# Expert feed-forward on one core: the gate times its sigmoid in one ScalarE function instead of a ScalarE sigmoid and a VectorE product

## What is computed

```
gu = xe @ w_gate_up[e] + b_gate_up[e]
gate, up = jnp.split(gu, 2, axis=-1)
gate = jnp.minimum(gate, SWIGLU_LIMIT)            # 7.0
up = jnp.clip(up, -SWIGLU_LIMIT, SWIGLU_LIMIT)
act = gate * jax.nn.sigmoid(SWIGLU_ALPHA * gate) * (up + 1)   # alpha = 1.702
y = act @ w_down[e] + b_down[e]
```

## Time and profile before

| | |
|---|---|
| time, median of 3 runs | 2448.58 us (2444.11 to 2453.59) |
| profiled execution, own time | 2447.04 us |
| its span | 2445.4 us |
| mean granted TensorE clock | 0.965 |
| PE busy | 2256.2 us (92%) |
| DVE busy | 1812.3 us (74%) |
| ACT busy | 1284.6 us (53%) |
| experts' stage | about 770 us to the end |

### The profile page before, as it was taken

The page is one execution under the profiler, slowest core; times in us unless marked ns, Lnnn a source line. Parts: engine busy times, 40 slices in busy tenths (PEclk is TensorE's granted clock), DMA queues, the critical chain, the costliest instruction groups (busy, mean ns, idle before and its releaser), DMA issues.

```text
span 2445.4 us, 37638 instructions
## 1 busy us (share of the span) xinstructions
PE 2256.2 (92%) x10569; PEld 1820.1 (74%) x10570; DVE 1812.3 (74%) x2326; ACT 1284.6 (53%) x1723; POOL 797.3 (33%) x780
## 2 busy tenths in 40 slices
PE   6899994897973999999999999999999999999997
PEld 2678883774862878888878888878778887878876
DVE  2784424674664799987789977787999878789797
ACT  2332211664323577755567655565777556566565
POOL 1253003892135134343223322231343322133141
PEclk9899997998985999999999999999999999999999
DMA  7134104972334799997679976696999868799695
GB/s 247 60 122 155 56 1 124 253 213 67 113 112 145 246 368 355 371 331 229 220 244 354 358 249 228 223 312 225 373 365 355 300 219 278 253 322 360 229 343 172
DMA packets 299173, 583.98 MB, mean 239 GB/s; under 512 B 23841, under 2 KB 53553, under 8 KB 297009
## 3 DMA queue, kind: packets, MB, share of 16 engines
q1 hardware_dynamic: 269200, 501.68, 59.3%
q0 software_dynamic: 26560, 69.06, 10.5%
q10 hardware_dynamic: 3362, 12.59, 1.4%
HBM read 544.79 MB, written 44.24 MB: 241 GB/s over the span
## 4 chain that ended last, share of the span: by engine, by line
PE 57%; DVE 6%; issue 4%; POOL 1%; DVEq 1%; ACT 0%; DMA 0%; POOLq 0%; ACTq 0%
PE psum L1936 51%; DVE d_wlo L1760 4%; PE psum L1918 2%; PE psum L1880 2%; PE psum L1888 2%; DVE d_up L1780 1%; DVE d_act L1786 1%; DVE d_glu L1767 1%; DVE d_atlo L1792 0%; ACT d_sg L1659 0%; DMA d_xg<-xn_d,d_entry 0%; POOL d_colf L1582 0%; POOL d_raw L1583 0%; DVEq L1759 0%; DVE d_y_two L1750 0%
## 5 line engine op out<-in xcount | busy, mean ns | idle before, releaser
L1760 DVE TENSOR_TENSOR d_wlo<-d_raw,d_whi 128x1024 fp32r<-128x1024 f32 x578 | 675.5, 1219 | 32.0 <-ACT d_whi L1637 30.4
L1637 ACT ACTIVATE d_whi<-d_raw 128x1024 fp32r<-128x1024 f32 x578 | 574.7, 1053 | 114.8 <-PE psum L1936 90.4
L1936 PE MATMUL psum<-d_whi,d_xthi 128*128 128x512 f32 x1152 | 459.2, 399 | 0.1
L1936 PE MATMUL psum<-d_whi,d_xtlo 128*128 128x512 f32 x1152 | 455.1, 395 | 0.0
L1936 PE MATMUL psum<-d_wlo,d_xthi 128*128 128x512 f32 x1152 | 455.0, 395 | 0.0
L1551 POOL DMA_INDIRECT out_dram<-d_yst,d_dest x49 | 94.2, 1922 | 844.1 <-DVE d_yst L1814 786.5
L1760 DVE TENSOR_TENSOR d_wlo<-slab,d_whi 128x1024 fp32r<-128x1024 f32 x292 | 343.7, 1219 | 4.5 <-ACT d_whi L1637 2.4
L1637 ACT ACTIVATE d_whi<-slab 128x1024 fp32r<-128x1024 f32 x292 | 292.5, 1054 | 6.0 <-PE psum L1936 5.6
L1936 PEld LDWEIGHTS psum<-d_whi,d_xtlo 128*128 128x128 f32 x1152 | 217.2, 189 | 50.7
L1936 PEld LDWEIGHTS psum<-d_whi,d_xthi 128*128 128x128 f32 x1152 | 217.3, 189 | 50.1 <-issue 1.4
L1936 PEld LDWEIGHTS psum<-d_wlo,d_xthi 128*128 128x128 f32 x1152 | 217.5, 189 | 48.3
(11 more groups left out here) (306 smaller groups left out, 4046.2 us busy)
## 6 DMA issues: line engine op xcount, KB each, us to landing
slab<-in_w_gate_up_dram SPq DMA_DIRECT2D x144, 1024.0 KB, 7.2
d_raw<-in_w_gate_up_dram SPq DMA_DIRECT2D x144, 1024.0 KB, 8.5
d_raw<-in_w_down_dram SPq DMA_DIRECT2D x144, 1024.0 KB, 6.3
b_wp<-in_w_ada_dram POOLq DMA_DIRECT2D x16, 1024.0 KB, 7.9
slab<-in_w_in_dram SPq DMA_DIRECT2D x12, 1024.0 KB, 5.3
slab<-in_w_ada_dram SPq DMA_DIRECT2D x8, 1024.0 KB, 5.1
b_q<-q_d SPq DMA_DIRECT2D x24, 256.0 KB, 8.0
b_k<-k_d SPq DMA_DIRECT2D x24, 256.0 KB, 8.8
```

Of the source, the lines that this page charges most:

```text
L1637: nc.scalar.activation(whi[n % NW][:, part, :], raw[n % NRAW][:, part, :], ACT.Copy).then_inc(whi_ok, 1)
L1760: nc.vector.tensor_tensor(wlo[n % NW][:, part, :], raw[n % NRAW][:, part, :], whi[n % NW][:, part, :].bitcast(F32), ALU.subtract).then_inc ...
L1936: mm = nc.tensor.matmul(to, m_[:, KH * h + k, :], w_[n % NW][:, k, :], start=(h == 0 and k == 0 and q == 0), stop=(h == 1 and k == KH - 1 ...
```

## The change

ACT evaluates one function, `Gelu_apprx_sigmoid`, which is x times sigmoid(1.702 x), instead of a sigmoid with the scale 1.702. The DVE product `d_glu` and its tile and semaphore go. The last DVE product limits the result of the function to CAP. PE's waits for a gate bank, and DVE's for the gate's part, are on `sg_ok`, which ACT raises. With two blocks DVE still sums `d_gate_two`.

```diff
-                def sigmoid(g, i, b, sh):
+                def gated(g, i, b, sh):
...
-                    nc.scalar.activation(sg[b][:, :], gate, ACT.Sigmoid, scale=ALPHA).then_inc(sg_ok, sh)
+                    nc.scalar.activation(sg[b][:, :], gate, ACT.Gelu_apprx_sigmoid).then_inc(sg_ok, sh)
...
-                nc.scalar.activation(sg[0][:, 0:1], s.eps[:, :], ACT.Sigmoid).then_inc(bhi_ok, 1)
+                nc.scalar.activation(sg[0][:, 0:1], s.eps[:, :], ACT.Gelu_apprx_sigmoid).then_inc(bhi_ok, 1)
...
-                def times_sigmoid(g, i, b, sh):
-
-                    dve.wait_ge(sg_ok, pair_count(g, i, b, sh))
-                    gate = psum[:, 2 * ((2 * i) % 3), :] if b == 0 else gate_two[:, :]
-                    nc.vector.scalar_tensor_tensor(glu[b][:, :], gate, LIMIT, sg[b][:, :],
-                                                   ALU.min, ALU.mult).then_inc(glu_ok, sh)
...
                 def activated(g, i, b, sh):
-                    dve.wait_ge(glu_ok, pair_count(g, i, b, sh))
+                    dve.wait_ge(sg_ok, pair_count(g, i, b, sh))
                     dve.wait_ge(up_ok, UP_CRED + pair_count(g, i, b, sh))
-                    nc.vector.scalar_tensor_tensor(act_t[b][0:ROWS[b], :], glu[b][:, :], CAP, up[b][:, :],
+                    nc.vector.scalar_tensor_tensor(act_t[b][0:ROWS[b], :], sg[b][:, :], CAP, up[b][:, :],
                                                    ALU.min, ALU.mult).then_inc(act_ok, sh)
...
-                        if n in (2, 6):
-                            if blocks == 2:
-                                gate_rows(g, n // 4)
-                            for b in range(blocks):
-                                times_sigmoid(g, n // 4, b, sh)
+                        if n in (2, 6) and blocks == 2:
+                            gate_rows(g, n // 4)
...
                     elif j == 3:
-                        pe.wait_ge(glu_ok, pair_count(g, 0, b, sh))
+                        pe.wait_ge(sg_ok, pair_count(g, 0, b, sh))
...
                     else:
-                        pe.wait_ge(glu_ok, pair_count(g, 1, b, sh))
+                        pe.wait_ge(sg_ok, pair_count(g, 1, b, sh))
```

More of the change, by code:

```diff
@@ L1392, in expert_block @@
         sg = [sb(f"d_sg{b}", [ROWS[b], SL], F32) for b in range(2)]
-        glu = [sb(f"d_glu{b}", [ROWS[b], SL], F32) for b in range(2)]
         up = [sb(f"d_up{b}", [ROWS[b], SL], F32) for b in range(2)]
@@ L1413, in expert_block @@
         xt_mm, xthi_ok, xt_ok = ([sem(f"d_{n}{b}") for b in range(2)] for n in ("xt_mm", "xthi_ok", "xt_ok"))
-        gu_mm, sg_ok, glu_ok, up_ok, act_ok = (sem("d_" + n) for n in ("gu_mm", "sg_ok", "glu_ok", "up_ok", "act_ok"))
+        gu_mm, sg_ok, up_ok, act_ok = (sem("d_" + n) for n in ("gu_mm", "sg_ok", "up_ok", "act_ok"))
         gate_low, up_low, y_low = (sem("d_" + n) for n in ("gate_low", "up_low", "y_low"))
@@ L1697, in body @@
                         if n in (2, 6):
-                            sigmoid(g, n // 4, 0, sh)
+                            gated(g, n // 4, 0, sh)
                             if blocks == 2:
                                 gate_rows(g, n // 4)
-                                sigmoid(g, n // 4, 1, sh)
+                                gated(g, n // 4, 1, sh)
                         if n in (4, 8) and blocks == 2:
```

## The result

| | before | changed |
|---|---|---|
| median | 2448.58 us (2444.11 to 2453.59, 5 runs) | 2427.96 us (2426.25 to 2433.17, 5 runs) |
| span of the profiled execution | 2445.4 us | 2426.2 us |
| mean granted clock | 0.965 | 0.967 |
| DVE busy, from 770 us on | 1401.5 us | 1342.1 us |

The ratio is 0.9921, with a 95% interval of 0.9908 to 0.9934: faster by 0.8%, 19 us by the ratio and 20.6 by the two medians. A later pair of medians, from runs of both kernels on one chip, was 2430.42 against 2447.84, ratio 0.9930 (0.9917 to 0.9944). The prediction was 2428.3.

What follows compares the result with a forecast made beforehand. PE was taken to bound the experts' stage, waiting almost only for DVE's `d_act`. 7.0 + 8.4 + 4.9 = 20.3 us, off 2448.6, gave 2428.3 us; the 8-in-10 range was 2422 to 2441.

Steps and rivals of the forecast that it cites:

- The place of the gain: PE's 20 waits for DVE's `d_act` at the transposes ahead of half 9, pair 1: 17.0 us, the whole prize.
- The term of 7.0 us: One-block groups starting an expert after a one-block group: 13 short stalls of 0.54 us go whole, 7.0 us.
- The term of 8.4 us: One-block groups after a two-block group: seven long stalls shrink by 1.20, from 2.01 to 0.81 us, 8.4 us.
- The clock, 4.9 us: Half-clock stretches on PE after three of seven long stalls all go: 3 x 1.65 = 4.9 us, bounds 0 and 4.9.
- The unseen operation: ACT's new function, absent from the trace, taken at the sigmoid's 595 ns for 128x512 from PSUM, bounds 595 to 684.
- The 0.2 us to spare: In the group without a stall, `d_act` ends about 0.2 us before the transposes start, covering a slightly dearer ACT function.
- B: Rival: ACT's function is dearer and its wait replaces DVE's ahead of half 9; 2436 to 2441 us, chance 0.10.
- C: Rival: nothing seen, another wait just behind or scatter hides the gain; 2448 with a few us either way, chance 0.10.
- D: Rival: slower, ACT's table switched inside the loop because copies lack the function's set; some 57 us more, 2506, chance 0.08.

Runs made afterwards that it cites:

- the second evaluation: Changed kernel with ACT evaluating the new function once more at n = 6 for the first block, into an unread tile: 2432.56 us, ratio 0.9942.
- The order alone: Kernel before, one-block groups: second instruction of half 10's split moved behind activated pair 1, half 11's behind transposed pair 1's low part; 2431.92 us, ratio 0.9943.

## Why the prediction was right

**The place of the gain.** It said that the whole prize is PE's 20 waits ahead of half 9. After the change 13 are gone and 7 are left, and three runs tie this to DVE's product alone: function without removal 1.0003, removal without function 0.9914, both products put back 1.0008.

**The term of 7.0 us.** The short stalls went, for the reason given: `d_act` starts 6.43 us behind ACT's split, DVE's split 1.09 behind it (forecast 6.43 and 1.10). That one product alone costs almost nothing in these groups, and two together the full stall, was shown by putting them back.

**The term of 8.4 us.** Forecast was that each of the seven shrinks by 1.20, from 2.01 to 0.81. By the distances, without the 0.3 us by which the lower clock lengthens one of them, the seven cost 14.2 us before and 5.8 after: 8.4 came back. It is an average of unlike groups: the one that the forecast was worked from shrank by 1.40, the other six by 1.08 to 1.24. Each product put back lengthened six of them by 0.55 to 0.6 us and that one by 0.8, and both together brought the 2.0 back.

**The clock, 4.9 us.** Taken at its upper bound, because the remaining stalls were nearer to the short ones. This held: no stretch follows any of the 146 stalls up to 1.7 us. The price of a stretch was right too: the three of the kernel before cost 5.1 us by the distances, and the stage takes 1671.2, 1669.0 and 1667.8 us in three kernels with the same stalls and three, two and one stretches. But the amount given back is that of the one profiled execution. Six of 21 stalls of 2.0 us had a stretch, on average 2 in a run of seven, worth 3.3 us and not 4.9, and over many executions this average is what counts. The sum is then 18.7 us, which is within the interval (16 to 23 us) as much as 20.3.

**The last digit is luck.** The median came within 0.4 us of the forecast. The profiled stage gave 21.7 us, 1.4 more than the sum, and the stages ahead took 2.5 more, of which the prediction says nothing; the second pair of medians differs by 17.4. What the runs confirm is the sum within 1 to 3 us, and its terms.

**The unseen operation.** 595 ns were taken and 594 measured. The 0.2 us to spare behind it, from one group's rows, was confirmed by the second evaluation: 0.47 us more on ACT cost 0.35 on PE, so 0.12 were to spare.

**The rivals.** B's mechanism exists, but needs a dearer function. C did not show. D didn't come about: the stage has one load, so the copies need no table but the new function's. Its price was put too high in one part: a load in a two-block group cost nothing, where I had bounds of 0 to 5.1 us each for four loads and took 1.7. With one load for each function, all 24 one-block groups stalled by 1.2 us, and the time was 27 us over the changed kernel's (25.7 in the stage). The full rival, two loads for each function, wasn't run.

**What I had not asked** is whether work has to go at all. The order alone gives the kernel before 14 of the 19 us, and 18 of the 22 in the stage.

## What to carry to other kernels

When a busy engine feeds the bound one, walk its queue back from the instruction that the bound engine waits for: only what stands there without a pause counts, and only down to the next producer's time. Moving an instruction behind the awaited one can be worth most of what removing one is, so try the order first, in small steps, and look at what else rides on that engine's pauses. A stall that is followed by a slower clock costs more than its length, but only in some executions, so count it over several profiles before it enters a sum. To compare two kernels, take the time of the changed stage as well as the medians: what stands ahead of it scatters by more than the terms of the sum.

## What the runs showed of the hardware

- `Gelu_apprx_sigmoid` of 128x512 from PSUM takes 594 ns, as the sigmoid and the copy do (595, 596). It is in another table than the sigmoid, and a copy needs no load under either.
- A table switch between two activations cost 1.44 us on ACT's timeline, of which the load is 1.28.
- PE stalls up to 1.7 us were never followed by a half-clock stretch (146 cases), those of 2.0 us in 6 of 21, those of 3.2 us in 5 of 7. A stretch cost 1.4 to 2.9 us by the distances.
- A wait costs PE more than the idle time that the trace shows: in a short stall 0.31 us idle stood for 0.54 us of distance. The trace counts idle time from 0.40 us after the last matmul's start, while without a stall the first transpose starts 0.24 after it; and the four transposes take 0.42 us instead of 0.35 up to the next matmul.
- GpSimd's scatter took 1.4 to 1.7 us where it met no split of DVE at its start, and 3.6, 5.3 or 9.86 us where it ended 1.5 us after a run of splits.
